# Splitting the up products of three attentions into high and low parts

## The chip, the cores and the metric

The kernel runs on one core of a Trainium2 chip. The metric is the device time of one launch in microseconds, as the median of several runs. The kernel before takes 1695.42 us (three runs, 1692.92 to 1697.69).

## What is computed

The reference runs two models one after the other on 256 tokens of width 1024. The first is one layer with a convolution mixer and a mixture of 32 experts. The second, which the change touches, has two layers. Each layer mixes three attentions, adds a cross attention over a memory, and a gated feed-forward block:

```python
for l in range(DEPTH_2):
    xn = rmsnorm_2(x, norm_mix[l])
    (qa, ka, va, qb, kb, vb, qc, kc, vc, qi, ki, wi, gates) = jnp.split(xn @ w_in[l], offsets, axis=-1)
...
    g = jax.nn.sigmoid(gates).reshape(b, s, 3, D_MODEL)
    y = (g[:, :, 0] * (o_a @ w_up_a[l]) + g[:, :, 1] * (o_b @ w_up_b[l])
         + g[:, :, 2] * (o_c @ w_up_c[l]))
    x = x + y @ w_out[l]
    x = x + memory_cross_attention(rmsnorm_2(x, norm_cross[l]), mem_n, w_q_x[l], w_kv_x[l], w_o_x[l])
    x = x + swiglu(rmsnorm_2(x, norm_ffn[l]), w_gu[l], w_down[l])
```

The attention results `o_a`, `o_b`, `o_c` are 256 x 512 each, the three `w_up` matrices 512 x 1024. `o_b` also passes an RMS norm per head (`subln`) before its up product. All of it is fp32.

## The kernel before

Activations are kept transposed: the 128 partitions are channels of a block, the free axis has 256 tokens. A product is a series of 128 x 128 weight tiles, each loaded into TensorE and streamed over by 256 columns of tokens.

There are two ways to make a product. A **direct** one multiplies fp32 by fp32; each such matmul of the program is issued as two instructions. A **split** one works on fp32r, a form of fp32 that one instruction multiplies at reduced precision. Both operands are written as a high part (a copy rounded to fp32r) and a low part (the value less the high part), and three products are added: high by high, low weight by high, high weight by low.

The weights come by DMA into three raw buffers in turn (`RAW = 3`; `raw_a` holds two, `raw_b` one), a piece of up to 2 MB at a time, in the order of the table `LAYER_PIECES`. `raw_free` says when a raw buffer may be overwritten: after a direct piece's product is done, after a split piece's last low part is written. A split piece is cut into chunks of 128 x 1024 values. For each chunk ScalarE copies the high part (`split`, `w_hi`), and VectorE subtracts to get the low part (`low`, `w_lo`, line 624). There are four chunk buffers (`PARTS = 4`), so that chunk n may be split only when TensorE has used chunk n - 4.

The order of everything in a layer is one list, `WORK`, which `with_splits` extends by the `split` and `low` steps. Each engine walks that list and issues its own part of each step, in order; semaphores tie them together. The queue of the weights is SyncE's.

The stage that the change touches comes behind the attentions. Twenty-four units of attention (a head pair by half of the tokens) run in overlapping steps: `scores` (TensorE), `exp` (VectorE lines 2322 and 2323, ScalarE line 1592), `probs` (VectorE, lines 2329 to 2337), `turn` and `apply` (TensorE lines 1457 and 1478, with ScalarE evacuations). Between them stand products for the six gates (`gates`, lines 973 to 976), which give TensorE work while a unit waits. Then:

- `subln_sums`, `subln`: the norm of the second attention. TensorE makes the sums (line 1487), ScalarE the root, VectorE the reciprocal and the scaling of `outs[:, 1]` (lines 2360 and 2361). ScalarE then makes the last gate.
- `("up", 16, 0)`, `("up", 17, 1)`, `("up", 18, 2)`: the three up products, direct ones (line 1506). Behind each half of a product VectorE multiplies by the gate (line 2374) and adds to the sum in `hT` (line 2379).
- After the last half ScalarE makes the high part of the sum (`h_hi`), VectorE the low part (`h_lo`, line 2388), and the product with `w_out` begins (`split_project`, line 1066). The trace calls `hT` by the name of its memory, `hs`.

The direct up product is this, with `outs[:, b]` the attention's result:

```python
for o in range(4):
    oo = half * 4 + o
    for k in range(4):
        last = mm(to[:, o, :], wu[:, k, oo * P:(oo + 1) * P], outs[:, b, k, :],
                  start=(k == 0), stop=(k == 3))
```

Of the kernel before, what the change touches and what calls it, by code (L numbers as in the profile page):

```python
# [18 lines left out]
P = 128  # L19
# [59 lines left out]
for _name, _width in (("norm_mix", KD), ("norm_cross", KD), ("norm_ffn", KD), ("subln", 1), ("lam_init", 1),  # L79
# [13 lines left out]
                + [("up", b) for b in range(3)] + [("out", 0), ("out", 1), ("kv_x",), ("q_x",), ("o_x",)]  # L93
# [5 lines left out]
def is_split(piece):  # L99


    return piece[0] in ("out", "gu", "down", "in", "q_x")
# [63 lines left out]
def without_last(steps, step):  # L166
# [22 lines left out]
def with_splits(work, layer):  # L189
# [6 lines left out]
    for w in work:  # L196
        used += {"proj": 4, "proj_v": 4, "out": 4, "gate_up": 4, "gates": 1, "down": 1, "index_proj": 3, "cross_q": 2}.get(w[0], 0)
# [32 lines left out]
        unit = unit or (w[0] == "rope" and w[1] >= 3)  # L230
# [5 lines left out]
        held = w[0] in ("gates", "probs", "scores", "turn", "apply", "cross_q", "square_b", "sums", "evac", "rope", "index_product", "subln_sums") or (w[0] == "exp" and w[1] >= 24)  # L236
# [11 lines left out]
        if direct_left and w[0] in ("up", "cross_v", "cross_o") and not (w[0] == "cross_v" and w[2] == 0):  # L248
            assert direct_left.pop(0) == w[1]
# [77 lines left out]
def build(nc, x, mem, cst, vec1, vec2, relpad, w_in, w_out, w1, w3, w2, w_in_2, w_up_a, w_up_b, w_up_c,  # L327
# [12 lines left out]
    with ExitStack() as ctx:  # L340
# [126 lines left out]
        o_of = {"A": outs[:, 0], "B": outs[:, 1], "C": outs[:, 2], "X": ox}  # L467
        otok = view(big, 0, TT, D)
# [4 lines left out]
        def small(*dims):  # L473
# [36 lines left out]
        (ident_in, up_half, consts_in, mem_in, squares_a, vec1_in, vec2_in, turned, sq_ready, sums_done, std_ready,  # L510
# [14 lines left out]
            "ident_in up_half consts_in mem_in squares_a vec1_in vec2_in turned sq_ready sums_done std_ready "  # L525
# [69 lines left out]
        def raw_of(i):  # L595
            return raw_a[:, i % RAW, :] if i % RAW < RAW - 1 else raw_b[:]
# [43 lines left out]
        def chunk_raw(n):  # L640


            i, o = chunk_source(n)
            if LAYER_PIECES[i][0] == "down":
                return view(raw_of(i), o * D, KD, P)
            width = {IDX: 3 * P, ("q_x",): SEQ}.get(LAYER_PIECES[i], HALF)
            whole = view(raw_of(i), 0, KD, width)
            return whole[:, 2 * o:2 * o + 2, :] if is_values(i) else whole[:, :, o * P:(o + 1) * P]
# [9 lines left out]
        def chunk_part(parts, n):  # L658
            i, _ = chunk_source(n)
            dims = (2, HALF) if is_values(i) else (KD, P)  # L660
            return view(parts[:, BUFFER[n], :], 0, *dims)
# [206 lines left out]
        def _(pe):  # L868
# [508 lines left out]
            for l in range(LAYERS):  # L1377
                for w in WORK:
# [111 lines left out]
                    elif kind == "up":  # L1490
                        i, b = w[1], w[2]
                        if b == 0:
                            freed(pe, "u_7", l)
                        elif b == 1:
                            pe.wait_ge(subln_ready, l + 1)
                        else:
                            freed(pe, "u_23", l)
# [12 lines left out]
                        last.then_inc(direct_done, 1)  # L1510
# [77 lines left out]
        def _(act_e):  # L1588
# [145 lines left out]
            for l in range(LAYERS):  # L1734
                for w in WORK_SPLIT[l]:
# [104 lines left out]
                    elif kind == "subln":  # L1840
                        act_e.wait_ge(sums_done, l * 4 + 2)
                        f(sq[:, 4:8], view(duo("subln"), 0, 4, SEQ), ACT.Sqrt, bias=eps[:]).then_inc(std_ready, 1)
                        saturate(whole_gate, l)
# [4 lines left out]
                    elif kind == "up" and w[2] == 2:  # L1848
                        for half in range(2):
                            act_e.wait_ge(mixed_ready, l * 2 + half + 1)  # L1850
                            f(h_hi[:, half * 4:half * 4 + 4, :], hT[:, half * 4:half * 4 + 4, :], ACT.Copy, scale=0.5
                              ).then_inc(h_hi_ready, 1)
# [27 lines left out]
        def _(v):  # L1880
# [316 lines left out]
            for l in range(LAYERS):  # L2197
                for w in WORK_SPLIT[l]:
# [158 lines left out]
                    elif kind == "subln":  # L2357
                        v.wait_ge(std_ready, l * 4 + 2)
                        v.sem_inc(free_of("subln"), 1)
                        link(v.reciprocal(sq[:, 4:8], sq[:, 4:8]))  # L2360
                        v.scalar_tensor_tensor(outs[:, 1], outs[:, 1], lam[:, 3:4], sq[:, 4:8], ALU.mult, ALU.mult
                                               ).then_inc(subln_ready, 1)
                    elif kind == "up":
                        b = w[2]
                        v.wait_ge(gates_ready, l * 6 + 2 * b + 2)
                        for half in range(2):
                            name = f"up_{b}_{half}"
                            if half == 0:
                                v.wait_ge(up_half, l * 3 + b + 1)
                            else:  # L2370
                                product_done(v, w[1], l)
# [6 lines left out]
                            if b:  # L2378
                                ins = v.tensor_tensor(y, y, term, ALU.add)
                                if b == 2:  # L2380
# [3 lines left out]
                        if b == 2:  # L2384
# [115 lines left out]
```

## Time and profile before

| | us |
|---|---|
| median of 3 runs | 1695.42 |
| the profiled execution | 1695.85 |
| its span | 1693.8 |
| TensorE busy in the span | 1603.3 (95%) |
| VectorE busy | 876.6 (52%) |
| ScalarE busy | 621.3 (37%) |
| on the chain that ended last: line 1506, the up products | 4.9% |

The profiled execution took 0.43 us more than the median. Its span begins with its first instruction and ends with its last. TensorE's busy time counts modelled ends of matmuls that overlap each other, so the spacing of the starts is what tells their cost.

### The profile page before, as it was taken

How to read it: one execution, taken by the hardware profiler on the slowest of the kernel's cores; microseconds unless marked ns; L12 is line 12 of the kernel's file. 1: busy time of each engine (PE TensorE's matmuls, PEld its weight loads, DVE VectorE, ACT ScalarE, POOL GpSimd, SP SyncE). 2: the span in 40 equal slices, each digit the busy share in tenths (PEclk: the TensorE clock that was granted, in tenths of full speed). 3: DMA queues.
4: the chain of work that ended last, by engine and by line, in shares of the span. 5: the costliest groups of instructions: out<-in, count | busy, mean ns of one | idle time of the engine just before them, and what ended most of it. 6: DMA issues, size and time to landing. Idle time of an engine off the chain costs nothing.

```text
span 1693.8 us, 25178 instructions
## 1 busy us (share of the span) xinstructions
PE 1603.3 (95%) x10739; PEld 1285.8 (76%) x10739; DVE 876.6 (52%) x1272; ACT 621.3 (37%) x990; POOL 58.1 (3%) x28
## 2 busy tenths in 40 slices
PE   8898989889989999998999899999999899899998
PEld 7785434443434479897788799999988788799998
DVE  6933212121211287678555676647668755476653
ACT  2123202111211154545514544435454542464443
POOL 0000000000000000060000000000015000000000
PEclk9988999999999999999999899999999999999999
DMA  9156999999999985426222655474634424256550
GB/s 351 66 212 258 427 430 428 428 428 428 430 429 426 423 298 181 140 103 221 100 102 98 211 187 174 163 256 158 216 105 150 147 78 174 94 181 199 174 188 37
DMA packets 126912, 393.78 MB, mean 232 GB/s; under 512 B 4320, under 2 KB 60000, under 8 KB 114016
## 3 DMA queue, kind: packets, MB, share of 16 engines
q1 hardware_dynamic: 126816, 392.38, 61.2%
q8 instruction: 74, 1.21, 0.3%
q14 instruction: 22, 0.18, 0.0%
HBM read 386.34 MB, written 1.05 MB: 229 GB/s over the span
## 4 chain that ended last, share of the span: by engine, by line
PE 66%; DVE 15%; DMA 10%; ACT 5%; issue 3%; SPq 0%; DVEq 0%; ACTq 0%
PE psum L1240 10%; DMA ring<-w 9%; PE psum L973 7%; PE psum L974 7%; PE psum L976 7%; PE psum L1506 5%; PE psum L1305 3%; DVE outs L1949 2%; ACT wp L1592 2%; PE psum L1573 2%; PE psum L1576 2%; PE psum L1575 2%; PE psum L1203 2%; PE psum L1004 2%; DVE score L2347 1%
## 5 line engine op out<-in xcount | busy, mean ns | idle before, releaser
L973 PE MATMUL psum<-h_hi,w_hi 128*128 128x256 f32 x1456 | 366.6, 289 | 1.8 <-ACT outs L1595 1.4
L974 PE MATMUL psum<-h_hi,w_lo 128*128 128x256 f32 x1456 | 361.5, 285 | 0.0
L973 PEld LDWEIGHTS psum<-h_hi,w_hi 128*128 128x128 f32 x1456 | 282.3, 194 | 7.3 <-issue 5.1
L974 PEld LDWEIGHTS psum<-h_hi,w_lo 128*128 128x128 f32 x1456 | 282.7, 194 | 0.2
L624 DVE TENSOR_TENSOR w_lo<-raw_a,w_hi 128x1024 fp32r<-128x1024 f32 x170 | 204.9, 1223 | 136.0 <-ACT w_hi L1595 135.1
L1595 ACT ACTIVATE w_hi<-raw_a 128x1024 fp32r<-128x1024 f32 x186 | 193.1, 1053 | 186.0 <-PE psum L976 70.2
L976 PE MATMUL psum<-h_lo,w_hi 128*128 128x256 f32 x1456 | 205.0, 284 | 0.0
L1240 PE MATMUL psum<-ring,outs 128*64 128x512 f32 x720 | 166.0, 617 | 27.3 <-DMA ring<-w 26.1
L976 PEld LDWEIGHTS psum<-h_lo,w_hi 128*128 128x128 f32 x1456 | 188.8, 193 | 0.0
L1240 PEld LDWEIGHTS psum<-ring,outs 128*64 128x64 f32 x720 | 58.0, 142 | 132.7 <-issue 132.7
L624 DVE TENSOR_TENSOR w_lo<-raw_b,w_hi 128x1024 fp32r<-128x1024 f32 x84 | 101.7, 1223 | 60.4 <-ACT w_hi L1595 59.7
L2150 DVE SCALAR_TENSOR_TENSOR qk<-psum,rtok,qk 128x512 f32<-128x512 f32 x16 | 18.2, 1138 | 220.2 <-PE psum L1240 220.2
L1595 ACT ACTIVATE w_hi<-raw_b 128x1024 fp32r<-128x1024 f32 x92 | 96.1, 1053 | 91.2 <-PE psum L976 56.0
L1305 PE MATMUL psum<-ring,qk 128*64 128x512 f32 x512 | 113.2, 594 | 0.0
L2143 DVE SCALAR_TENSOR_TENSOR moe_parts<-psum,rtok,moe_parts 128x512 fp32r<-128x512 f32 x34 | 24.1, 746 | 141.4 <-ACT moe_parts L1592 141.4
L1573 PE MATMUL psum<-act_parts,w_hi 128*128 128x256 f32 x328 | 92.2, 281 | 0.0
L1575 PE MATMUL psum<-act_parts,w_hi 128*128 128x256 f32 x328 | 92.2, 281 | 0.0
L1576 PE MATMUL psum<-act_parts,w_lo 128*128 128x256 f32 x328 | 92.1, 281 | 0.0
L1595 ACT ACTIVATE qk<-psum 128x512 f32<-128x512 f32 (+1 forms) x26 | 16.4, 631 | 196.1 <-PE psum L1283 164.0
L1305 PEld LDWEIGHTS psum<-ring,qk 128*64 128x64 f32 x512 | 36.9, 137 | 62.7 <-issue 62.6
L624 POOL TENSOR_TENSOR w_lo<-raw_a,w_hi 128x1024 fp32r<-128x1024 f32 x16 | 38.7, 2449 | 1232.7 <-ACT w_hi L1595 1232.7
L1592 ACT ACTIVATE wp<-wp,stat 128x256 f32<-128x256 f32 (+1 forms) x112 | 50.9, 455 | 62.6 <-DVE stat L2323 62.5
(298 smaller groups left out, 2516.4 us busy)
## 6 DMA issues: line engine op xcount, KB each, us to landing
ring<-w SPq DMA_DIRECT2D x76, 2048.0 KB, 16.6
raw_a<-w_in SPq DMA_DIRECT2D x20, 2048.0 KB, 8.2
raw_a<-w_gu SPq DMA_DIRECT2D x32, 1024.0 KB, 7.8
raw_b<-w_in SPq DMA_DIRECT2D x10, 2048.0 KB, 8.4
wp<-w SPq DMA_DIRECT2D x8, 2048.0 KB, 18.7
hs<-w SPq DMA_DIRECT2D x8, 2048.0 KB, 23.1
raw_b<-w_gu SPq DMA_DIRECT2D x12, 1024.0 KB, 7.5
raw_a<-w_down SPq DMA_DIRECT2D x8, 1536.0 KB, 6.6
```

What stands on the lines that cost most here:

```text
L624: return eng.tensor_tensor(chunk_part(w_lo, n), chunk_raw(n), chunk_part(w_hi, n).bitcast(F32), ALU.subtract)
L973: mm(to, hi[:, k, :], h_hi[:, k, :], start=(k == 0), stop=False)
L974: mm(to, lo[:, k, :], h_hi[:, k, :], start=False, stop=False)
L976: last = mm(to, hi[:, k, :], h_lo[:, k, :], start=False, stop=(k == KD - 1))
L1240: last = mm(psum[rows, d, bank * 512:bank * 512 + 512], duo_tokens[k // 4][:, k % 4, cols], view(places[e], 0, KD, D_EXPERT)[:, k, :], sta ...
L1305: last = mm(psum[rows, 2, half * 512:half * 512 + 512], hidT[:, f, rows], view(ring[:, at + e, :], 0, 4, D)[:, f, half * 512:half * 512 + ...
L1506: last = mm(to[:, o, :], wu[:, k, oo * P:(oo + 1) * P], outs[:, b, k, :], start=(k == 0), stop=(k == 3))
L1573: mm(to, hi[:, o, :], act_hi[:, k, :], start=(k == 0 and o % 2 == 0), stop=False, skip_group_check=True)
L1575: mm(to, hi[:, o, :], act_lo[:, k, :], start=False, stop=False, skip_group_check=True)
L1576: last = mm(to, lo[:, o, :], act_hi[:, k, :], start=False, stop=(k == KF - 1), skip_group_check=True)
L1592: return nca.activation(out_ap, in_ap, func, **kw)
L1595: return nca.activation(out_ap, in_ap, ACT.Copy)
```

## The change

The three up products become split ones.

- `is_split` now counts the `up` pieces as split: each has four chunks of 128 x 1024 (all 512 input channels by 256 output channels), and a layer has 151 chunks where it had 139.
- The order of the products becomes first, third, second attention, and with it the order in which their weights are loaded.
- The results of the attentions get a high part (`outs_high`, a copy on ScalarE) and a low part (`outs_low`, a subtraction on VectorE, now line 2390), kept in memory that other steps leave free here (`act_lo`, `h_hi`, `h_lo`). Those of the first attention are made at unit 19, of the third after the last `apply`, of the second after its norm.
- The reciprocal of the norm is cut in two halves with the low part of a chunk between them, and the last gate is made after the first product.
- The sum of the first half is finished inside the last product (`up_add`), with its high part behind it (`mixed_high`).

```diff
-                + [("up", b) for b in range(3)] + [("out", 0), ("out", 1), ("kv_x",), ("q_x",), ("o_x",)]
+                + [("up", b) for b in (0, 2, 1)] + [("out", 0), ("out", 1), ("kv_x",), ("q_x",), ("o_x",)]
-    return piece[0] in ("out", "gu", "down", "in", "q_x")
+    return piece[0] in ("up", "out", "gu", "down", "in", "q_x")
-                                         20: [("gates", 14, 4, 3), ("square_b",)]},
-                                  {13: [("rope", 3, "qc")], 14: [("rope", 4, "kc")]}), ("apply", 23))
-        + [("subln_sums",), ("apply", 23), ("subln",)] + [("up", 16 + b, b) for b in range(3)]
+                                         19: [("outs_high", 0), ("gates", 14, 4, 2)], 20: [("gates", 14, 4, 3), ("square_b",)]},
+                                  {13: [("rope", 3, "qc")], 14: [("rope", 4, "kc")], 19: [("outs_low", 0)]}), ("apply", 23))
+        + [("subln_sums",), ("apply", 23), ("outs_high", 2), ("outs_low", 2), ("subln",), ("subln_rest",), ("up", 16, 0),
+           ("gate_last",), ("outs_high", 1), ("outs_low", 1), ("up", 17, 2), ("up", 18, 1)]
+        for _ in range({"subln_sums": used + PARTS - split, "subln_rest": 1}.get(w[0], 0)):
+            out += [("split", split), ("low", split)]
+            split += 1
+        if w == ("up", 18, 1):
+            for n, then in enumerate(([], [("up_add", 1, 0)], [("mixed_high", 0)], [])):
+                out += [("split", split + n), ("low", split + n)] + then
+            split += 4
...
+        out_hi = [act_lo[:, 8:12], act_lo[:, 0:4], h_hi[:, 4:8]]
+        out_lo = [act_lo[:, 12:16], act_lo[:, 4:8], h_lo[:, 4:8]]
+        part_turn = {0: 1, 2: 2, 1: 3}
...
-                        raw_arrived(pe, i, l)
-                        wu = view(raw_of(i), 0, 4, D)
-                        for half in range(2):
-                            enter(pe, f"up_{b}_{half}", l)
-                            to = view(duo(f"up_{b}_{half}"), 0, 4, SEQ)
-                            for o in range(4):
-                                oo = half * 4 + o
+                        for q in range(4):
+                            n = SPLIT_THROUGH[i] - 4 + q
+                            if q % 2 == 0:
+                                enter(pe, f"up_{b}_{q // 2}", l)
+                            parts_ready(pe, n, l)
+                            hi, lo = chunk_part(w_hi, n), chunk_part(w_lo, n)
+                            pe.wait_ge(outs_hi_ready, l * 3 + part_turn[b])
+                            for o in range(2):
+                                to = view(duo(f"up_{b}_{q // 2}"), 0, 4, SEQ)[:, q % 2 * 2 + o, :]
                                 for k in range(4):
-                                    last = mm(to[:, o, :], wu[:, k, oo * P:(oo + 1) * P], outs[:, b, k, :],
-                                              start=(k == 0), stop=(k == 3))
-                            if half == 0:
-                                last.then_inc(up_half, 1)
-                        last.then_inc(direct_done, 1)
+                                    mm(to, hi[:, k, o * P:(o + 1) * P], out_hi[b][:, k, :], start=(k == 0), stop=False)
+                                    mm(to, lo[:, k, o * P:(o + 1) * P], out_hi[b][:, k, :], start=False, stop=False)
+                                pe.wait_ge(outs_lo_ready, l * 3 + part_turn[b])
+                                for k in range(4):
+                                    last = mm(to, hi[:, k, o * P:(o + 1) * P], out_lo[b][:, k, :], start=False,
+                                              stop=(k == 3))
+                            last.then_inc(chunk_used, 1)
...
+                    elif kind == "outs_high":
+                        b = w[1]
...
+                        copy(out_hi[b], outs[:, b]).then_inc(outs_hi_ready, 1)
+                    elif kind == "gate_last":
                         saturate(whole_gate, l)
                         whole_gate = None
...
-                        link(v.reciprocal(sq[:, 4:8], sq[:, 4:8]))
+                        link(v.reciprocal(sq[:, 4:6], sq[:, 4:6]))
+                    elif kind == "subln_rest":
+                        link(v.reciprocal(sq[:, 6:8], sq[:, 6:8]))
...
+                    elif kind == "outs_low":
+                        b = w[1]
+                        v.wait_ge(outs_hi_ready, l * 3 + part_turn[b])
+                        v.tensor_tensor(out_lo[b], outs[:, b], out_hi[b].bitcast(F32), ALU.subtract).then_inc(outs_lo_ready, 1)
-                        for half in range(2):
+                        for half in (0, 1) if i < 18 else (int(kind == "up"),):
                             name = f"up_{b}_{half}"
-                            if half == 0:
-                                v.wait_ge(up_half, l * 3 + b + 1)
-                            else:
-                                product_done(v, w[1], l)
+                            v.wait_ge(chunk_used, l * N_CHUNKS + SPLIT_THROUGH[i] + PARTS - 2 + 2 * half)
```

VectorE, from the end of unit 23 of the first of the two layers to the first chunks of `w_out`, before (line 624 is a low part of a chunk, 2360 the reciprocal, 2361 the scaling, 2374 and 2379 gate and sum, 2388 the low part of the sum):

```order
L2337 TENSOR_TENSOR wp<-wp,stat 128x512
L2274 TENSOR_TENSOR big<-psum,rstd 128x512
L2360 RECIPROCAL hs<-hs 128x1024
L2361 SCALAR_TENSOR_TENSOR outs<-outs,lam,hs 128x1024
L2374 SCALAR_TENSOR_TENSOR hs<-big,psum 128x1024 x2
L624 TENSOR_TENSOR w_lo<-raw_a,w_hi 128x1024 x3
L2374 SCALAR_TENSOR_TENSOR hs<-big,psum 128x1024
L2379 TENSOR_TENSOR hs<-hs 128x1024
```

The same stretch of VectorE in the changed kernel, from the same instruction on (line 635 is the low part of a chunk, 2390 that of an attention's result, 2399 and 2404 gate and sum):

```order
L2359 TENSOR_TENSOR wp<-wp,stat 128x512
L635 TENSOR_TENSOR w_lo<-raw_a,w_hi 128x1024
L2296 TENSOR_TENSOR big<-psum,rstd 128x512
L635 TENSOR_TENSOR w_lo<-raw_a,w_hi 128x1024 x2
L2390 TENSOR_TENSOR h_lo<-outs,h_hi 128x1024
L2382 RECIPROCAL hs<-hs 128x512
L635 TENSOR_TENSOR w_lo<-raw_b,w_hi 128x1024
L2384 RECIPROCAL hs<-hs 128x512
L2385 SCALAR_TENSOR_TENSOR outs<-outs,lam,hs 128x1024
L635 TENSOR_TENSOR w_lo<-raw_b,w_hi 128x1024 x2
L2399 SCALAR_TENSOR_TENSOR hs<-big,psum 128x1024 x2
L2390 TENSOR_TENSOR act_parts<-outs,act_parts 128x1024
```

Three low parts of chunks now stand ahead of the reciprocal, where there was none, and three more ahead of the first gate product.

What follows on VectorE in the changed kernel, down to the low parts of the sum (line 2413):

```order
L635 TENSOR_TENSOR w_lo<-raw_b,w_hi 128x1024
L635 TENSOR_TENSOR w_lo<-raw_a,w_hi 128x1024 x3
L2399 SCALAR_TENSOR_TENSOR hs<-big,psum 128x1024
L2404 TENSOR_TENSOR hs<-hs 128x1024
L2399 SCALAR_TENSOR_TENSOR hs<-big,psum 128x1024
L2404 TENSOR_TENSOR hs<-hs 128x1024
L635 TENSOR_TENSOR w_lo<-raw_a,w_hi 128x1024 x2
L2399 SCALAR_TENSOR_TENSOR hs<-big,psum 128x1024
L2404 TENSOR_TENSOR hs<-hs 128x1024
L635 TENSOR_TENSOR w_lo<-raw_a,w_hi 128x1024 x2
L2399 SCALAR_TENSOR_TENSOR hs<-big,psum 128x1024
L2404 TENSOR_TENSOR hs<-hs 128x1024
```

Eight low parts of chunks now stand between the gate products of the three attentions, where three stood before.

ScalarE in the changed kernel, from the last two evacuations of the attentions (`outs<-psum`) to the first high part of the sum:

```order
L1606 ACTIVATE outs<-psum 128x128
L1606 ACTIVATE w_hi<-raw_a 128x1024 x2
L1606 ACTIVATE outs<-psum 128x128
L1606 ACTIVATE h_hi<-outs 128x1024
L1603 ACT_TABLE_LOAD
L1603 ACTIVATE hs<-psum,eps 128x1024
L1606 ACTIVATE w_hi<-raw_b 128x1024 x3
L1603 ACT_TABLE_LOAD
L1603 ACTIVATE big<-big 128x1024
L1606 ACTIVATE act_parts<-outs 128x1024
L1606 ACTIVATE w_hi<-raw_b 128x1024
L1606 ACTIVATE w_hi<-raw_a 128x1024 x6
```

The high part of the third attention's result (`h_hi<-outs`) now stands ahead of the root (`hs<-psum,eps`), and the last gate (`big<-big`) behind three chunks.

## Rows read from the trace of the kernel before

**Rows 1.** The page of the profile: span, then busy time, share and count of each engine

```profile
span 1693.8 us, 25178 instructions
PE 1603.3 (95%) x10739; PEld 1285.8 (76%) x10739; DVE 876.6 (52%) x1272; ACT 621.3 (37%) x990; POOL 58.1 (3%) x28
```

**Rows 2.** The chain that ended last, first layer then second: start us, us, what

```profile
845.85 41.69 PE psum L1506 x192
...
887.57 1.24 DVE hs L2374
...
888.83 1.23 DVE hs L2379
890.05 1.15 DVE h_lo L2388
...
1382.68 41.69 PE psum L1506 x192
...
1428.07 1.94 PE psum L1066 x14
```

**Rows 3.** Stretches of TensorE: us, busy (count of matmuls), granted clock, DMA share, GB/s

```profile
814.00:818.00 4.00, 4.00 (x23) 0.57 0.74 213
...
1347.00:1351.00 4.00, 2.31 (x18) 0.91 0.01 2
1351.00:1355.00 4.00, 4.00 (x24) 0.66 0.69 225
...
891.00:895.00 4.00, 3.76 (x31) 1.00 1.01 380
...
1100.00:1140.00 40.00, 40.00 (x340) 1.00 0.69 238
```

**Rows 4.** Timeline of VectorE, first layer: start us, us, what [idle before <- releaser]

```profile
837.45 0.69 DVE L2322 SCALAR_TENSOR_TENSOR wp<-psum,wp 128x512 f32<-128x512 f32 x1 [0.59 <-PE psum L1447]
...
840.23 0.69 DVE L2337 TENSOR_TENSOR wp<-wp,stat 128x512 f32<-128x512 f32 x1
...
848.28 6.55 DVE L2360 RECIPROCAL hs<-hs 128x1024 f32<-128x1024 f32 x1 [6.12 <-ACT hs L1592]
854.87 1.28 DVE L2361 SCALAR_TENSOR_TENSOR outs<-outs,lam,hs 128x1024 f32<-128x1024 f32 x1
...
868.86 3.50 DVE L624 TENSOR_TENSOR w_lo<-raw_a,w_hi 128x1024 fp32r<-128x1024 f32 x3 [7.63 <-ACT w_hi L1595]
```

**Rows 5.** Timeline of ScalarE, first layer

```profile
836.02 0.19 ACT L1592 ACTIVATION_READ_ACCUMULATOR wp<-wp,stat 128x1 f32 x1
...
845.43 0.28 ACT L1595 ACTIVATE outs<-psum 128x128 f32<-128x128 f32 x1 [2.76 <-PE psum L1478]
...
849.45 1.06 ACT L1592 ACTIVATE big<-big 128x1024 f32<-128x1024 f32 x1
```

**Rows 6.** Timeline of TensorE: idle stretches ahead of a matmul, and turns of units

```profile
812.78 0.66 PE L1457 MATMUL psum<-consts,wp 128*128 128x128 f32 x4 [1.58 <-DVE wp L2337]
...
841.27 0.60 PE L1457 MATMUL psum<-consts,wp 128*128 128x128 f32 x4
...
891.24 1.70 PE L1066 MATMUL psum<-h_lo,w_hi 128*128 128x256 f32 x12 [0.85 <-DVE h_lo L2388]
...
1349.62 0.66 PE L1457 MATMUL psum<-consts,wp 128*128 128x128 f32 x4 [1.69 <-DVE wp L2337]
```

**Rows 7.** Groups by line in 845.5 to 891.5 us: busy us, mean ns, idle before

```profile
L2374 DVE SCALAR_TENSOR_TENSOR hs<-big,psum 128x1024 f32<-128x1024 f32 x6 | 7.3, 1219 | 10.6 <-PE psum L1506 10.6
...
L2379 DVE TENSOR_TENSOR hs<-hs 128x1024 f32<-128x1024 f32 x4 | 4.9, 1225 | 0.1
...
L1595 ACT ACTIVATE w_hi<-raw_a 128x1024 fp32r<-128x1024 f32 x4 | 4.0, 1048 | 17.2 <-DMA raw_a<-w_out 17.2
```

**Rows 8.** Timeline of SyncE's queue, first layer: issues of weight pieces

```profile
833.94 0.37 SPq L853 DMA_DIRECT2D raw_a<-w_up_c  x1
...
859.93 0.37 SPq L853 DMA_DIRECT2D raw_a<-w_out  x1
```

More of the change, by code:

```diff
@@ L196, in with_splits @@
     for w in work:
-        used += {"proj": 4, "proj_v": 4, "out": 4, "gate_up": 4, "gates": 1, "down": 1, "index_proj": 3, "cross_q": 2}.get(w[0], 0)
+        used += {"proj": 4, "proj_v": 4, "up": 4, "out": 4, "gate_up": 4, "gates": 1, "down": 1, "index_proj": 3, "cross_q": 2}.get(w[0], 0)
         unit = w[0] in ("scores", "probs", "turn", "apply", "gates", "exp", "square_b")
@@ L229, in with_splits @@
             out.append(("root", first))
-        unit = unit or (w[0] == "rope" and w[1] >= 3)
+        unit = unit or (w[0] == "rope" and w[1] >= 3) or w in (("outs_high", 0), ("outs_low", 0))
         if unit:
@@ L235, in with_splits @@
             low = []
-        held = w[0] in ("gates", "probs", "scores", "turn", "apply", "cross_q", "square_b", "sums", "evac", "rope", "index_product", "subln_sums") or (w[0] == "exp" and w[1] >= 24)
+        held = w[0] in ("gates", "probs", "scores", "turn", "apply", "cross_q", "square_b", "sums", "evac", "rope", "index_product", "subln_sums", "outs_high", "outs_low", "subln", "subln_rest") or (w[0] == "exp" and w[1] >= 24)
+        for _ in range({"subln_sums": used + PARTS - split, "subln_rest": 1}.get(w[0], 0)):
[5 more added lines that the diff above has]
+            split += 4
         while (not held and split < N_CHUNKS and split < used + PARTS - 1
@@ L247, in with_splits @@
             out.append(w)
-        if direct_left and w[0] in ("up", "cross_v", "cross_o") and not (w[0] == "cross_v" and w[2] == 0):
+        if direct_left and w[0] in ("cross_v", "cross_o") and not (w[0] == "cross_v" and w[2] == 0):
             assert direct_left.pop(0) == w[1]
@@ L645, in chunk_raw @@
                 return view(raw_of(i), o * D, KD, P)
+            if LAYER_PIECES[i][0] == "up":
+                return view(raw_of(i), 0, 4, D)[:, :, 2 * P * o:2 * P * (o + 1)]
             width = {IDX: 3 * P, ("q_x",): SEQ}.get(LAYER_PIECES[i], HALF)
@@ L659, in chunk_part @@
             i, _ = chunk_source(n)
-            dims = (2, HALF) if is_values(i) else (KD, P)
+            dims = (2, HALF) if is_values(i) else (4, 2 * P) if LAYER_PIECES[i][0] == "up" else (KD, P)
             return view(parts[:, BUFFER[n], :], 0, *dims)
@@ L1842, in _ @@
                         f(sq[:, 4:8], view(duo("subln"), 0, 4, SEQ), ACT.Sqrt, bias=eps[:]).then_inc(std_ready, 1)
+                    elif kind == "outs_high":
+                        b = w[1]
+                        if b == 0:
+                            freed(act_e, "u_7", l)
+                        elif b == 1:
+                            act_e.wait_ge(subln_ready, l + 1)
+                        else:
+                            freed(act_e, "u_23", l)
+                            product_done(act_e, 15, l)
+                        copy(out_hi[b], outs[:, b]).then_inc(outs_hi_ready, 1)
+                    elif kind == "gate_last":
                         saturate(whole_gate, l)
@@ L1847, in _ @@
                         copy(qx, view(duo("xq"), 0, 2, SEQ)).then_inc(free_of("xq"), 1)
-                    elif kind == "up" and w[2] == 2:
-                        for half in range(2):
-                            act_e.wait_ge(mixed_ready, l * 2 + half + 1)
-                            f(h_hi[:, half * 4:half * 4 + 4, :], hT[:, half * 4:half * 4 + 4, :], ACT.Copy, scale=0.5
-                              ).then_inc(h_hi_ready, 1)
+                    elif kind == "mixed_high" or w == ("up", 18, 1):
+                        half = 0 if kind == "mixed_high" else 1
+                        act_e.wait_ge(mixed_ready, l * 2 + half + 1)
+                        f(h_hi[:, half * 4:half * 4 + 4, :], hT[:, half * 4:half * 4 + 4, :], ACT.Copy, scale=0.5
+                          ).then_inc(h_hi_ready, 1)
                     elif kind == "cross_k":
@@ L2383, in _ @@
                                     link(ins)
[L2384 removed]
+                        if w == ("up", 18, 1):
                             for half in range(2):
```

17 lines of the change are left out of this document (5 added, 12 removed).

## The prediction, made before the changed kernel ran

> **What bounds the kernel now.** I read the page first. TensorE is busy 95% of the span, VectorE 52%, ScalarE 37% [rows 1]. The three up products matter, then, if they are time in which nothing else could have gone on. The chain of waits says so: in each layer 192 instructions of line 1506 stand in it without a gap, for 41.69 us [rows 2]. The stretch ends in a tail that no product covers. When the last up product is done at 887.54, VectorE multiplies by the gate from 887.57, adds from 888.83, and writes the low part of the sum from 890.05; only then, at 891.24, may TensorE go on with the low products of `w_out` [rows 2, 6]. From the first up matmul to that point it is 891.24 - 845.85 = 45.39 us. The second layer has the same: 1428.07 - 1382.68 = 45.39 us. I take this length as what the change works on, and look for what ends last in it.
>
> **The products themselves.** The direct product has 96 matmuls of the program per layer and takes 41.69 us, 434 ns each. The split one has 3 x 96 = 288 fp32r matmuls of the same 128 x 256 shape. What such a one costs where TensorE has nothing to wait for is in the feed-forward stretch: 340 in 40 us at full clock, so 117.6 ns each [rows 3]. That is 288 x 0.1176 = 33.9 us, or 2.82 us for a chunk of 24. TensorE alone would gain 41.7 - 33.9 = 7.8 us per layer. Whether it can have them depends on VectorE, which must now write a low part for each chunk.
>
> **The work ahead of the stage.** Unit 19 gets a copy on ScalarE and a subtraction on VectorE, each of about the size of the nearest rows, 1.05 and 1.22 us [rows 7]. VectorE waits there for ScalarE as in every unit, and TensorE has gate products; I cost it at nothing. The cover is that gate product, and without it the price is 1.2 us. Unit 22 gets a chunk to split, where there was none. ScalarE is free at 836.02 + 0.19 = 836.21 [rows 5]; with 1.05 us for the high and 1.22 for the low part VectorE comes to the scores of unit 23 at 838.5 instead of 837.45 [rows 4]. Of these 1.05 us 0.35 are slack, since VectorE ends the unit's last step at 840.23 + 0.69 = 840.92, and TensorE takes it up at 841.27 [rows 4, 6]. So the attentions end 0.7 us later, and the first up matmul comes at 846.55. The bounds of this step are 0 and the whole 2.3 us of both halves of the split. The three further chunks lie in VectorE's and ScalarE's pauses of 6.12 and 2.76 us ahead of the norm [rows 4, 5].
>
> **VectorE from the norm on.** It starts the reciprocal at 848.28 now [rows 4]. It will be later by the 0.7 us and by ScalarE's copy of the third result, 1.05 us, which stands ahead of the root: 850.0. From there to the last gate product nearly all of its work is in a row. The pieces:
>
> - the reciprocal in two halves, together 6.55 us, and the scaling, 1.28 us [rows 4]
> - eleven low parts of chunks, eight of the stage's twelve and the first three of `w_out`; three in a row take 3.50 us, 1.17 each [rows 4]: 12.9 us
> - one low part of a result that stands in this row: 1.22 us
> - eight gate products and sums at 1.22 us each and 0.03 between them [rows 7]: 10.0 us
> - a wait of some 0.9 us for the high part of the third chunk of `w_out`, since ScalarE first makes the high part of the half sum (1.06 + 1.05 us, against 1.17 on VectorE)
>
> The sum is 32.8 us, so the last gate product may begin at 882.8. TensorE would be through the last chunk at 846.55 + 33.9 = 880.4. **VectorE ends last**, by 2.4 us, and the tail follows as it does now: 891.24 - 887.57 = 3.67 us. TensorE goes on with the low products of `w_out` at 886.5 instead of 891.24. That is a gain of 4.75 us per layer.
>
> Does TensorE starve before that? The sixth chunk's low part comes at 860.2 and is wanted at 846.55 + 5 x 2.82 = 860.65; the eighth's comes at 866.3, behind both gate products of the first attention and a low part, and is wanted at 866.3; the twelfth's comes at 876.0 and is wanted at 877.6. The margins are 0.4, 0 and 1.6 us, and a small miss is covered by the 2.4 us at the end.
>
> **The clock.** TensorE's pause in the tail grows. It is 0.85 us now [rows 6]. In the changed kernel it ends the last chunk at 880.4, has 24 high products of `w_out` for 2.8 us, and then waits for 886.5: 3.3 us. The rows show what shorter pauses do. Behind one of 1.58 us the granted clock is 0.57 in 814 to 818, behind one of 1.69 us it is 0.91 and 0.66 in the next two stretches [rows 3, 6]. Both times that is 1.7 us of work lost (4 x 0.43, and 4 x 0.09 + 4 x 0.34), with TensorE at the lower of its two levels, 1.2 GHz, for a few microseconds. Behind the pause of 0.85 us the clock is 1.00 [rows 3, 6]. The bounds are 0 and two such falls, 3.4 us; I take one, 1.7 us, which all lies on the path, since TensorE is busy from there on. A net gain of 3.05 us per layer is left.
>
> The Trainium skill speaks of this in "TensorE: Matmul & The Clock Gate", section "HAM oscillation — how this bites in real kernels": only gaps above a size that is larger than the pause I expect are said to matter. By it the 1.7 us would not be paid. The trace has the clock fall behind pauses half as long, so I follow the trace.
>
> **Edits that cost nothing.** The order first, third, second puts the norm under two products. Its weights come in the same queue, and the third attention's is wanted only when a chunk of the first is used, at 846.55 + 2.8 us. The pieces behind come earlier: a split piece frees its raw buffer with its last low part, so that the first half of `w_out` can be issued near 847 instead of 859.93 [rows 8]. It was not waited for by TensorE before, so nothing is gained. The later last gate is wanted only with the second product, and the larger count of chunks shifts numbers only.
>
> **Sum.** 2 x 3.05 = 6.1 us. Against the profiled execution, 1695.85, that is 1689.75; against the median of 1695.42, which is 0.43 lower, **1689.3**.
>
> **The rivals.** A measurement of this kernel can tell about 0.3% from no change, 5.1 us, so faster means below 1690.3.
>
> - *The clock holds in the tail.* For it speaks that 24 matmuls stand between the last chunk and the pause; against it both falls behind shorter pauses. Gain 2 x 4.75 = 9.5: 1685.9. Without the delay of the attentions too, 1684.5.
> - *The attentions pay.* Unit 23 has TensorE waiting for VectorE longer than I think, 1.7 instead of 0.7 us, and such a pause lowers the clock there as well. Each layer gains 4.75 - 1.7 - 1.0 - 1.7 = 0.35: 1694.7, no change that can be told. For it speaks that the rows with a fall are just such waits of a turn for VectorE.
> - *Starvation at the product's ends, slower.* Where a low part stands behind the gate products, TensorE has nothing until three instructions of VectorE are through: 1.25 + 1.22 + 1.17 = 3.65 us at the end of the first product, as much at the second's. This decides if VectorE falls some 3 us further behind, so that it has no chunk ready ahead. Each such stop also lowers the clock, 1.7 us. TensorE ends at 880.4 + 2 x 5.35 = 891.1, the tail adds 3.67 and its own fall 1.7: 896.5, which is 5.2 us behind the kernel before, and 1705.9 in all. Against it speak the low parts of the fifth to seventh chunk, which need only buffers.
>
> **How the numbers follow.** My forecast gets 0.43, the held clock 0.27, the paying attentions 0.18, starvation 0.12. The forecast lies 1.0 us under the line of 1690.3 and may miss it by a small error; I count a fifth of it as no change. Faster is 0.34 + 0.27 and a little of the third, 0.62; no change 0.26; slower 0.12. The range leaves out the slower rival and the ends of the others: from 1684.5 to 1695.5.
>
> **What would show it.** In the changed profile the up matmuls should start 118 ns apart, 288 to a layer, with the chain of waits passing from TensorE to VectorE near the stage's end: the last gate product should wait not for TensorE but for the low part ahead of it. From the first up matmul to the first low product of `w_out` it should be 886.5 - 846.55 = 40 us instead of 45.4. TensorE should pause some 3 us there, and the clock should be near 0.6 in the next 4 us. Pauses of 3.7 us inside the stage would show starvation; an unchanged clock behind the tail, the first rival; a stage of 45 us or more, that I am wrong about VectorE's row.

## The result, and the profile after

The changed kernel takes **1686.5 us** in the median of five runs (1684.6 to 1687.6), against 1695.42. The ratio is 0.9948, with a 95% interval of 0.9932 to 0.9963: faster by 0.5%. I had said 1689.3 us, from 1684.5 to 1695.5.

The page of the changed kernel, to be read beside [rows 1]:

```profile
span 1685.5 us, 25656 instructions
PE 1593.2 (95%) x10931; PEld 1285.6 (76%) x10931; DVE 910.9 (54%) x1304; ACT 651.8 (39%) x1020; POOL 58.1 (3%) x28
```

TensorE has 192 instructions more and is busy 10 us less. VectorE and ScalarE are busy 34 and 30 us more. The span is 8.3 us shorter.

What ends last in the stage is in the chain of waits of its end, first layer. The columns are start, duration and what. It answers to [rows 2], where the products stood in the chain up to 887.54:

```profile
876.14 0.66 DVE w_lo L635
876.80 0.48 issue
877.28 1.22 DVE w_lo L635
878.50 1.14 DVE hs L2399
879.64 0.02 issue
879.66 1.24 DVE hs L2404
880.90 0.02 issue
880.92 1.06 ACT h_hi L1603
881.99 0.95 ACT w_hi L1606
882.94 0.02 issue
882.96 0.04 DVE w_lo L635
883.00 1.11 issue
884.11 1.23 DVE hs L2399
885.33 0.02 issue
885.36 1.23 DVE hs L2404
886.58 1.15 DVE h_lo L2413
887.73 0.04 issue
887.77 4.24 PE psum L1079 x21
```

TensorE has left the chain. VectorE's low parts, gate products and sums follow on each other, and the last gate product, at 884.11, waits for a low part of `w_out`, which has waited for ScalarE. On TensorE's timeline the same end reads so (start, duration, what, and the idle time before it with what ended it); it answers to [rows 6]:

```profile
881.77 0.64 PE L1519 MATMUL psum<-act_parts,w_hi 128*128 128x256 f32 x4
882.25 1.59 PE L1079 MATMUL psum<-h_hi,w_hi 128*128 128x256 f32 x12
883.68 1.60 PE L1079 MATMUL psum<-h_hi,w_lo 128*128 128x256 f32 x12
887.77 1.44 PE L1079 MATMUL psum<-h_lo,w_hi 128*128 128x256 f32 x5 [2.49 <-DVE h_lo L2413]
```

The last chunk is through at 882.25, the gate product begins 1.9 us later, and TensorE pauses for 2.49 us. The first up matmul of this profile is at 847.92, so the stage is 887.77 - 847.92 = 39.85 us, where it was 45.39. The second layer has 1421.09 - 1381.25 = 39.84 us.

The clock behind the pause, in stretches of TensorE (us, busy and count, granted clock, DMA share, GB/s), for both layers:

```profile
887.00:891.00 4.00, 3.23 (x15) 0.59 0.00 0
891.00:895.00 4.00, 4.00 (x35) 0.99 0.79 266
...
1418.00:1422.00 4.00, 1.52 (x13) 1.00 0.03 10
1422.00:1426.00 4.00, 4.00 (x36) 1.00 0.32 84
```

It fell in the first layer and not in the second.

### The profile page after: what moved, and what is told of

It is laid out like the page before. It is cut to its first block, busy times and chain, and to the rows that moved or that the text cites. A ratio compares the mean times of both kernels' runs of the same rounds, so it can differ in the third digit from the quotient of the medians.

```text
span 1685.5 us, 25656 instructions
## 1 busy us (share of the span) xinstructions
PE 1593.2 (95%) x10931; PEld 1285.6 (76%) x10931; DVE 910.9 (54%) x1304; ACT 651.8 (39%) x1020; POOL 58.1 (3%) x28
## 4 chain that ended last, share of the span: by engine, by line
PE 61%; DVE 18%; DMA 10%; ACT 6%; issue 4%; SPq 0%; DVEq 0%; ACTq 0%
PE psum L1253 10%; DMA ring<-w 9%; PE psum L986 7%; PE psum L987 7%; PE psum L989 7%; PE psum L1318 3%; ACT wp L1603 3%; DVE outs L1971 3%; DVE w_lo L635 2%; PE psum L1586 2%; PE psum L1584 2%; PE psum L1587 2%; PE psum L1216 2%; PE psum L1017 2%; DVE stat L2345 2%
## 5 line engine op out<-in xcount | busy, mean ns | idle before, releaser
L635 DVE TENSOR_TENSOR w_lo<-raw_a,w_hi 128x1024 fp32r<-128x1024 f32 x186 | 224.1, 1223 | 125.1 <-ACT w_hi L1606 124.0
L1606 ACT ACTIVATE w_hi<-raw_a 128x1024 fp32r<-128x1024 f32 x202 | 210.2, 1053 | 169.5 <-PE psum L989 70.4
L635 DVE TENSOR_TENSOR w_lo<-raw_b,w_hi 128x1024 fp32r<-128x1024 f32 x92 | 111.3, 1223 | 62.0 <-ACT w_hi L1606 61.2
L1606 ACT ACTIVATE w_hi<-raw_b 128x1024 fp32r<-128x1024 f32 x100 | 104.5, 1053 | 99.3 <-PE psum L989 56.1
```

The costliest lines, as they stand in the source:

```text
L635: return eng.tensor_tensor(chunk_part(w_lo, n), chunk_raw(n), chunk_part(w_hi, n).bitcast(F32), ALU.subtract)
L1606: return nca.activation(out_ap, in_ap, ACT.Copy)
```

## The experiments

All ratios are to the kernel before, run on the same chip. The stage is always measured from the first up matmul to the first low product of `w_out`. Its length agrees between the two layers of a profile within 0.01 us, except where two lengths are given, and between two profiles of one kernel, so one profile tells 0.1 us there. The whole time of one kernel scatters by 1 to 7 us between executions.

**The changed kernel again.**

> The changed kernel once more, as the yardstick for the others. Expected near 1686.5 us. The stage from the first up matmul to the first low product of w_out should be 39.8 to 39.9 us in both layers again if VectorE's row sets it. The granted clock behind the pause of TensorE at the stage's end fell in one layer of two in the first profile; if that is a matter of chance, it may fall in none, one or both here, each for some 1.5 us.

Measured: 1687.3 us, ratio 0.9947 (0.9933 to 0.9960). The stage is 39.85 and 39.84 us. The clock fell behind the pause in the first layer and not in the second.

**Less work for TensorE.**

```diff
-                                    mm(to, lo[:, k, o * P:(o + 1) * P], out_hi[b][:, k, :], start=False, stop=False)
```

> Leaves out a third of the up products: the low part of the weights by the high part of the results is not multiplied. TensorE has 192 matmuls per layer in the stage instead of 288, 11.3 us less. Theory (VectorE's row of low parts, reciprocals and gate products sets the stage): the stage stays at 39 to 40 us, and the whole within 2 us of the changed kernel, apart from falls of the clock that the longer pauses bring. Rival (TensorE's 33.9 us and its waits set it): the stage shrinks by 5 to 11 us per layer, the whole by 10 to 20 us.

The first up matmul, a stop in the second product, and the first low product of `w_out` on TensorE's timeline:

```profile
847.49 0.74 PE L1515 MATMUL psum<-act_parts,w_hi 128*128 128x256 f32 x4 [0.39 <-ACT outs L1605]
...
861.49 0.74 PE L1515 MATMUL psum<-h_hi,w_hi 128*128 128x256 f32 x4 [3.52 <-DVE w_lo L635]
...
887.32 2.93 PE L1079 MATMUL psum<-h_lo,w_hi 128*128 128x256 f32 x12 [2.59 <-DVE h_lo L2412]
```

The stage is 39.83 us in both layers, and the whole 1687.25 us, ratio 0.9949 (0.9931 to 0.9967). Taking a third of the matmuls away, 11 us per layer, changes nothing: TensorE spends that time in stops, among them 3.52, 1.83 and 1.71 us for low parts of chunks. TensorE does not bound the stage.

**One instruction more for VectorE.**

```diff
+                        if b == 1:
+                            link(v.tensor_tensor(out_lo[b], outs[:, b], out_hi[b].bitcast(F32), ALU.subtract))
                         v.tensor_tensor(out_lo[b], outs[:, b], out_hi[b].bitcast(F32), ALU.subtract).then_inc(outs_lo_ready, 1)
```

> Makes the low part of the second attention's result twice, one 128 x 1024 instruction more on VectorE in its row. Theory: the stage is longer by its 1.25 us in both layers, 41.1 us, the whole by 2.5 us. Rival (VectorE has slack in the stage): no change.

```profile
846.34 0.38 PE L1515 MATMUL psum<-act_parts,w_hi 128*128 128x256 f32 x1 [0.39 <-ACT outs L1606]
...
887.43 1.70 PE L1079 MATMUL psum<-h_lo,w_hi 128*128 128x256 f32 x12 [2.56 <-DVE h_lo L2415]
```

The stage is 887.43 - 846.34 = 41.09 us, and 41.09 in the second layer: 1.24 us longer for an instruction of 1.25 us. VectorE has no slack in this row. The whole is 1688.3 us, ratio 0.9952 (0.9933 to 0.9971). Against the 0.9947 of the changed kernel on another chip that is 0.8 us more instead of the 2.5 expected, a difference that the intervals can't tell.

**Three low parts on GpSimd.**

```diff
-POOL_CHUNKS = range(SPLIT_THROUGH[8], SPLIT_THROUGH[11])
+POOL_CHUNKS = [*range(SPLIT_THROUGH[8], SPLIT_THROUGH[11]), *range(SPLIT_THROUGH[18], SPLIT_THROUGH[18] + 3)]
...
                 parts_ready(eng, SPLIT_THROUGH[before] - 1, l, int(i < RAW))
+                last = SPLIT_THROUGH[before] - 1
+                others = [n for n in range(last - chunks_of(LAYER_PIECES[before]) + 1, last)
+                          if (n in POOL_CHUNKS) != (last in POOL_CHUNKS)]
+                if others:
+                    assert i >= RAW
+                    parts_ready(eng, others[-1], l)
```

> The low parts of the first three chunks of w_out are made by GpSimd instead of VectorE. VectorE's row loses 3 x 1.17 us and the wait of 0.9 us for the high part, 4.4 us per layer; then TensorE ends last (34 us) and the stage is 34 + 3.7 = 37.7 us instead of 39.85. The pause of TensorE at the end goes back to about 0.9 us, so the clock should not fall behind it. Theory: 4.3 us less for both layers, and 0 to 3 us for the clock, 1679 to 1683 us. Rival (TensorE's order of waits sets the stage, not VectorE): no change. Second rival (GpSimd's 2.45 us per chunk come too late, or slow VectorE down): the same or slower than 1686.5.

Measured: 1685.4 us, ratio 0.9938 (0.9924 to 0.9952), and a stage of 40.64 us in both layers, longer instead of 2 us shorter. The timelines of GpSimd and of VectorE tell why:

```profile
874.61 6.46 POOL L635 TENSOR_TENSOR w_lo<-raw_a,w_hi 128x1024 fp32r<-128x1024 f32 x2 [115.53 <-ACT w_hi L1612]
884.38 2.43 POOL L635 TENSOR_TENSOR w_lo<-raw_a,w_hi 128x1024 fp32r<-128x1024 f32 x1 [3.30 <-ACT w_hi L1612]
```

```profile
875.52 3.31 DVE L635 TENSOR_TENSOR w_lo<-raw_a,w_hi 128x1024 fp32r<-128x1024 f32 x1
878.75 1.21 DVE L2405 SCALAR_TENSOR_TENSOR hs<-big,psum 128x1024 f32<-128x1024 f32 x1
879.99 2.17 DVE L2410 TENSOR_TENSOR hs<-hs 128x1024 f32<-128x1024 f32 x1
882.09 1.22 DVE L2405 SCALAR_TENSOR_TENSOR hs<-big,psum 128x1024 f32<-128x1024 f32 x1
883.34 1.23 DVE L2410 TENSOR_TENSOR hs<-hs 128x1024 f32<-128x1024 f32 x1
884.49 4.54 DVE L2419 SCALAR_TENSOR_TENSOR h_lo<-hs,h_hi 128x1024 fp32r<-128x1024 f32 x2
```

While GpSimd subtracts, VectorE's low part takes 3.31 us instead of 1.22, a sum 2.17 and two low parts of the sum 4.54 instead of 2.43. The gate product at 878.75, which reads one operand from PSUM, keeps its 1.21 us. The second rival had it right: the 4.4 us taken off VectorE's row came back as 2.09 + 0.94 + 2.11 = 5.1 us in slower neighbours, and the stage grew by 0.8 us. The clock did not fall in either layer; there the long pause was gone.

**The pause filled.** Twenty matmuls whose result nobody reads, ahead of the wait for the low part of the sum:

```diff
+                enter(pe, "out_1", l)
+                spare = view(duo("out_1"), 0, 4, SEQ)
+                for n in range(20):
+                    mm(spare[:, 0, :], chunk_part(w_hi, chunk[0])[:, n % 4, :], h_hi[:, n % 4, :], start=True, stop=True,
+                       skip_group_check=True)
                 pe.wait_ge(h_lo_ready, base + 1)
```

> Adds 20 fp32r matmuls (2.4 us) to TensorE in the pause at the stage's end, into a region of PSUM that the next product overwrites; nothing waits for them. Theory of the clock (the pause of 3 us lets the granted clock fall): the stage stays at 39.85 us, the pause shrinks to about 1 us, and the clock stays at 1.00 behind it in both layers, so the whole is 0 to 3 us below the changed kernel, 1.5 us if the clock fell in one layer of two. Rival (the falls have nothing to do with this pause): no change, and falls as before.

```profile
887.00:891.00 4.00, 3.92 (x33) 1.00 0.02 4
891.00:895.00 4.00, 4.00 (x36) 1.00 0.82 264
...
1418.00:1422.00 4.00, 3.92 (x32) 1.00 0.00 0
1422.00:1426.00 4.00, 4.00 (x36) 1.00 0.65 200
```

The stage keeps its 39.84 us in both layers, and the clock stays at 1.00 behind it in both. The whole is 1685.0 us (1682.2 to 1687.9), 2.3 us below the changed kernel on the same chip. The ratio, 0.9934 (0.9919 to 0.9950), overlaps that of the changed kernel, so the gain is in the expected direction and not shown by the times alone. Since the clock fell in only one layer of two without the filling, two stages without a fall don't prove by themselves that the filling is the reason either.

**The reciprocal in one piece.**

```diff
-                        link(v.reciprocal(sq[:, 4:6], sq[:, 4:6]))
+                        link(v.reciprocal(sq[:, 4:8], sq[:, 4:8]))
...
-                        link(v.reciprocal(sq[:, 6:8], sq[:, 6:8]))
```

> The reciprocal is one instruction again instead of two halves with the low part of the fifth chunk between them. VectorE's work is the same. The fifth chunk's low part comes 3.35 us later, at about 859.4 us of the first profile, which is when TensorE wants it. Theory: no change, the stage within 0.4 us of 39.85. Rival (the halves keep TensorE from starving): TensorE stops at the fifth chunk, and the stage grows by 1 us or more.

```profile
849.79 0.39 PE L1515 MATMUL psum<-act_parts,w_hi 128*128 128x256 f32 x1 [0.39 <-ACT outs L1606]
...
889.44 1.70 PE L1079 MATMUL psum<-h_lo,w_hi 128*128 128x256 f32 x12 [2.15 <-DVE h_lo L2412]
```

The stage is 39.65 us, 0.2 us shorter. TensorE loses only 0.15 us at the fifth chunk (from its first up matmul to `w_out` it takes 34.48 us instead of 34.33), which lies under VectorE's row. The halves buy nothing here; they cost their second start (3.35 + 3.35 us against 6.55). The clock fell in neither layer behind a pause of 2.15 us. The whole is 1685.2 us, ratio 0.9935 (0.9917 to 0.9953).

**The old order of the products.** First, second, third, all else as in the changed kernel:

```diff
-                + [("up", b) for b in (0, 2, 1)] + [("out", 0), ("out", 1), ("kv_x",), ("q_x",), ("o_x",)]
+                + [("up", b) for b in (0, 1, 2)] + [("out", 0), ("out", 1), ("kv_x",), ("q_x",), ("o_x",)]
...
-           ("gate_last",), ("outs_high", 1), ("outs_low", 1), ("up", 17, 2), ("up", 18, 1)]
+           ("gate_last",), ("outs_high", 1), ("outs_low", 1), ("up", 17, 1), ("up", 18, 2)]
```

> The changed kernel with the old order of the products, first, second, third. The second attention's result is then wanted some 11.4 us after the first up matmul, at 859.5 us in the first profile; its high part is ready at 861.8 and its low part at 866.7 us. Theory: TensorE stops for 5 to 7 us in each layer, its last chunk ends 6 us later, beyond VectorE's row, and the stage is 43 to 46 us; with a fall of the clock behind the stop the whole is 1694 to 1702 us, the gain of the change gone. Rival (the order is of no account, since VectorE ends last anyway): the stage stays within 1 us of 39.85.

```profile
859.94 0.36 PE L1515 MATMUL psum<-act_parts,w_hi 128*128 128x256 f32 x1 [2.42 <-DVE w_lo L635]
...
864.68 1.22 PE L1519 MATMUL psum<-act_parts,w_hi 128*128 128x256 f32 x4 [3.56 <-DVE act_parts L2390]
```

```profile
863.00:867.00 4.00, 2.32 (x11) 0.50 0.04 6
867.00:871.00 4.00, 4.00 (x30) 0.83 0.99 342
```

TensorE stops twice, 2.42 and 3.56 us, at the start of the second attention's product. The first stop ends with the high part of that attention's result, which ScalarE finishes at 859.80 (the profile names a low part that ended beside it), the second with its low part. Behind the first stop the granted clock falls, to 0.50 in 863 to 867, which is 1.2 GHz. The stage is 47.19 and 46.96 us, more than the 43 to 46 expected: in the first layer TensorE comes to `w_out` 42.46 us behind its first up matmul, which is its 34.33 us, the two stops of 5.98 us, and 2.15 us that I put down to the lower clock and had left out. The whole is 1697.9 us, ratio 1.0013 (1.0002 to 1.0024): no better than the kernel before, if anything a little worse. Without the new order the split gains nothing. Of the other parts of the change, the later last gate, the early parts of the first attention's result and the half sum inside the last product were not taken back one by one.

**A low part moved behind the sum.** In the changed kernel VectorE is ready for the last gate product 1.9 us after TensorE, because of one low part that `w_out` needs only later:

```diff
-                out += [("split", split + n), ("low", split + n)] + then
+                out += [("split", split + n)] + ([("low", split + n)] if n < 3 else []) + then
...
+        if w == ("up", 18, 1):
+            out.append(("low", split - 1))
...
                 pe.wait_ge(h_hi_ready, base + 2)
-                for o in range(3):
+                for o in range(2):
                     products(o, halves[1], [w_hi, w_lo], h_hi)
+                parts_ready(pe, chunk[2], l)
+                products(2, halves[0], [w_lo], h_hi)
+                products(2, halves[1], [w_hi, w_lo], h_hi)
```

The loop of the first low products runs over two chunks likewise.

> Moves the low part of the third chunk of w_out on VectorE from ahead of the last gate product to behind the low parts of the sum; TensorE multiplies with it later, too. In the changed kernel VectorE is ready for the last gate product 2.1 us after TensorE has ended the last chunk: 1.2 us for this low part and 0.9 us of waiting for its high part. Theory (VectorE's row ends last): the last gate product begins with the end of TensorE's last chunk, the stage goes from 39.85 to 37.8 us in both layers, the pause of TensorE to about 1 us or 1.5 us, so the clock falls less or not: 4.1 us, and up to 3 us more by the clock, 1680 to 1683 us. Rival: TensorE then waits for this low part behind the sum, and the 2 us come back there: no change.

VectorE around the last gate product:

```profile
879.05 1.22 DVE L637 TENSOR_TENSOR w_lo<-raw_a,w_hi 128x1024 fp32r<-128x1024 f32 x1
880.78 1.22 DVE L2404 SCALAR_TENSOR_TENSOR hs<-big,psum 128x1024 f32<-128x1024 f32 x1 [0.51 <-PE psum L1524]
```

The gate product now waits for TensorE, 0.51 us. The stage is 38.27 us in both layers, the pause 1.40 us, and the clock holds in both. The whole is 1683.2 us, ratio 0.9923 (0.9908 to 0.9937). Of the 2.1 us expected per layer 1.6 came, since TensorE's last chunk ends 34.3 us after its first matmul and not 34.0, and the gate product begins 0.27 us behind that (880.51 to 880.78).

**The delay ahead of the stage.**

```diff
-        while (not held and split < N_CHUNKS and split < used + PARTS - 1
+        while (not held and w != ("exp", 22) and not (w == ("exp", 23) and split > SPLIT_THROUGH[15])
+               and split < N_CHUNKS and split < used + PARTS - 1
```

> The chunk that the changed kernel splits within unit 22 is split in unit 23, and that of unit 23 behind the last apply, with two others; nothing else moves. The first up matmul comes 0.5 us later in each layer of the changed kernel than in the kernel before, if the part ahead of it is taken off. Theory: this is the split of unit 22, which holds up the scores of unit 23 on VectorE; without it the first up matmul comes 0.4 to 0.5 us earlier in each layer, 1 us in all, and the stage keeps its 39.85 us. Rival (ScalarE's three splits in a row hold up the evacuation of the last apply instead): no change, or 0.5 us later.

As a mark ahead of the stage I take the last rope sum of VectorE, in unit 17, which the change leaves alone. Before, in the changed kernel, and in the one with all three edits below:

```profile
795.73 1.22 DVE L2296 TENSOR_TENSOR qk<-qk,hs 128x1024 f32<-128x1024 f32 x1
```

```profile
797.25 1.22 DVE L2318 TENSOR_TENSOR qk<-qk,hs 128x1024 f32<-128x1024 f32 x1
```

```profile
797.06 1.21 DVE L2324 TENSOR_TENSOR qk<-qk,hs 128x1024 f32<-128x1024 f32 x1
```

From there to the first up matmul it is 845.85 - 795.73 = 50.12 us before and 847.92 - 797.25 = 50.67 us after; in the second layer 50.01 and 50.55. The units cost 0.55 us per layer. With the chunks split later it is 49.30 and 49.89 us, and the stage keeps its 39.84 us. In the second layer, where the clock fell as in the changed kernel, the 0.55 us are back. Of the 1.4 us of the first layer some 0.7 are the clock's: the granted clock was 1.00 through this whole stretch, where it fell in the kernel before and in the changed one. It was 1.00 there with the filled pause, too, which changes nothing ahead of the stage, and the stretch took 49.94 us instead of 50.67. The whole is 1685.8 us, ratio 0.9952 (0.9935 to 0.9969), which tells nothing by itself.

**The three edits together:** the late low part, the later chunks, the reciprocal in one piece.

> Three edits together: the late low part of the third chunk of w_out, the chunks of units 22 and 23 split later, and the reciprocal in one instruction. Theory: TensorE ends last, so the stage stays at 38.3 us, as with the late low part alone, and the 0.2 us of the whole reciprocal, which lie in VectorE's row, no longer count; the first up matmul comes 0.5 us earlier in each layer. The whole is 1 us below the late low part alone, 1681 to 1683 us. Rival: with the whole reciprocal the fifth chunk comes too late once the stage begins earlier, and the stage grows by 0.5 us or more.

```profile
847.08 0.39 PE L1521 MATMUL psum<-act_parts,w_hi 128*128 128x256 f32 x1 [0.39 <-ACT outs L1612]
...
885.50 1.69 PE L1082 MATMUL psum<-h_lo,w_hi 128*128 128x256 f32 x12 [1.40 <-DVE h_lo L2418]
```

Measured: **1680.6 us** (1678.6 to 1681.4), ratio 0.9919 (0.9903 to 0.9934). That is faster than the later chunks alone, 1685.8 us on the same chip. The late low part alone had a ratio of 0.9923 on another chip; the two can't be told apart. The way to the stage is 847.08 - 797.06 = 50.02 us, and 49.90 in the second layer, as before the change. The stage is 38.42 us instead of 38.27. The 0.15 us that the whole reciprocal costs TensorE at the fifth chunk count once the stage is TensorE's. With the halves left in, the stage should be 38.27 us again; that was not run.

## Why the prediction was right, step by step

- **What bounds the stage.** Right. VectorE's row ends last in the changed kernel. A third of TensorE's work less gave 0.01 to 0.02 us, one VectorE instruction more gave its 1.24 us.
- **The row's length.** Right by 0.1 us. From the first up matmul to the low products of `w_out` I had 886.5 - 846.55 = 39.95 us; it is 39.85. The single terms are near, too. The row begins at 851.54 - 847.92 = 3.6 us behind the first up matmul, where I had 3.45, and a half of the reciprocal takes 3.35 us where I had 3.28. The last gate product comes 884.11 - 847.92 = 36.2 us behind it, as the 882.8 - 846.55 of the sum.
- **No starvation.** Right. TensorE's chunks began 0.4, 0.2 and 2.1 us behind the low parts of the sixth, eighth and twelfth chunk, where I had 0.4, 0 and 1.6. A forecast margin of 0 is luck as much as reckoning: the sum did not say how long TensorE would stop if it missed.
- **TensorE's own time.** I took 117.6 ns for each matmul, from the feed-forward stretch. From 847.92 to 882.25 it is 34.33 us for 288, or 119 ns. So the margin between the two engines was 1.9 us, not 2.4.
- **The attentions.** I had 0.7 us per layer, measured are 0.55. The later split of the two chunks points to their share in it.
- **The clock: mis-sized.** The step "I take one, 1.7 us" per layer failed in its count: one fall came in two layers. In the eight stages whose last pause was 2.48 to 2.56 us (the changed kernel twice, one instruction more, the later chunks; two layers each) the clock fell in four, once in each profile, for some 1.7 us of work. In the twelve with shorter last pauses, up to 2.15 us, or with filled ones, it fell in none behind that pause. (In two of these twelve, with the old order, it had fallen before, behind the longer stops within the stage. The kernel with a third of the matmuls left out has further pauses of 2.5 us, had a fall near the end of both stages, and isn't counted.) A fall in every layer had been inferred from pauses of 1.58 and 1.69 us in the attentions [rows 3, 6], but 2.15 us went without one here, and so did the very turn of the attentions behind which [rows 3] has 0.57: with the filled pause and with the later chunks its pause was 1.70 and 1.69 us and the clock stayed at 1.00 behind it. What the clock follows is more than the last pause. The page of the Trainium skill that I weighed against the rows ("TensorE: Matmul & The Clock Gate", section "HAM oscillation — how this bites in real kernels") names only longer gaps than these as harmful. The four falls speak against taking it as a bound, the four stages without one against my taking the rows as one.
- **The pause.** I had 3.3 us and it is 2.49. TensorE ended 0.5 us later than in my sum, and its 24 high products took 3.0 us instead of 2.8.

With the measured sizes the sum is 2 x (45.39 - 39.85) = 11.1 us, less 2 x 0.55 for the attentions and 1.7 for one fall, which makes 8.3 us; the span shrank by 8.3 us. Other stretches moved as well and cancel in that: the second model began 1.5 us later, in work that the change doesn't touch, and the cross attention of the second layer went 1.3 us faster, behind a shorter fall of the clock. So the close agreement of the sum with the span is in part luck. Against my 6.1 us the span gave 2.2 us more: 1.7 of them are the fall that did not come, 0.5 the stage and the attentions. The median fell by 8.9 us; the 0.6 us beyond the span's are within the scatter.

Of the rivals, *the clock holds in the tail* happened in one layer of two. *The attentions pay* did not: no added stop of 1.7 us there. *Starvation* did not happen in this order of the products, but is real: with the old order TensorE stops for 6.0 us and the time is 1697.9 us, and what was late there was the norm of the second attention, not a chunk. The price per stop that I had given, 3.65 us and a fall of 1.7 us, was near the measured one (2.42 and 3.56 us, and 2.15 us for the clock for both together).

## What to carry to other kernels

When a cheaper product needs its operands prepared, cost the preparing engine's whole row between two fixed points, instruction by instruction, before believing the gain of TensorE: here TensorE's work for the products shrank by 7.4 us per layer (41.69 to 34.33), and the stage by 5.5 us. Then look at the row's end: an instruction there that nobody needs yet costs its full length, and moving one low part gave 1.6 us per layer. A clock that may or may not fall behind a pause belongs into the range and not, at full price, into the forecast.

## What the runs showed of the hardware

GpSimd and VectorE hold each other up when both work on two operands in SBUF. VectorE's 128 x 1024 low part went from 1.22 to 3.31 us, while a gate product with one operand in PSUM kept its 1.21 us. The starts and ends read as if one waits for the other's whole instruction. In the first layer GpSimd's three low parts end at 877.74, 881.08 and 886.81, and the three slowed VectorE instructions end 1.09, 1.08 and 1.08 us behind these, at 878.83, 882.16 and 887.89, which is about the time that one takes alone. GpSimd's first two took 3.13 and 3.38 us instead of 2.43, and end 2.25 us behind the VectorE instruction beside which they began. In the second layer it is the same within 0.01 us. No other run tests this reading. The Trainium skill has this in "GPSIMD Engine Reference", section "Specifications", which lists the interfaces to SBUF as shared with VectorE, with contention for instructions of two SBUF inputs; the runs agree, and 0.9 to 2.1 us for one instruction is the size they show. I had looked at GpSimd's own 2.45 us for a chunk, and not at what it does to its neighbour.
